# A two-layer attention and state-space block on one core: filter products, chunk outputs and key transposes laid out differently on the TensorE array

## The chip, the cores and the metric

The kernel runs on one core of one Trainium2 chip. The metric is device time in microseconds (us) of one execution. It is written by hand for each engine: every engine has its own list of instructions, and semaphores (`S["name"]`, counted up by `then_inc` and waited for by `wait_ge`) order them against each other.

## The reference

The input is 512 tokens of width 1024. A first layer modulates and normalises them, projects them, and mixes two branches: an attention branch (compressed, selected and window keys) and a state-space branch. Two further layers with neighbourhood attention and differential attention follow, then a last normalisation. The part that is changed lies in the first layer, above all in the state-space branch. There, 32 groups of 16 channels each carry a complex state of 64 values; the 512 tokens are cut into chunks of 8 tokens. In the kernel's form, each group's output is

```
y[group] = toe[group]^T . u[group]   (inside a chunk: a 128 x 128 block-triangular filter)
         + cl[group]^T  . st[group]  (what the state at the start of the chunk adds)
```

with u and st 128 x 64 (64 chunks). The filter blocks in `toe` come from small products kk[group] = b_st[group]^T . cl[group], 16 x 128, which DMAs then copy into a shifted pattern. The state `st` comes from v[group] = w[group]^T . u[group], a rotation, and a scan over the chunks.

## The kernel before

All matmuls of interest here have fp32 operands; the trace holds two records for each such matmul and one for each transpose. The bulk of the projections runs on a high and a low part of each operand (fp32r), three matmuls of 512 columns for each 128 x 128 piece of a weight.

TensorE's order around the change is written out (lines 1112 to 1264): the projections KV and KW (`proj_tok`, 96 matmuls each); 32 transposes of the state weights (L1119 to L1126); the 32 kk products (L1132 to L1137), whose outputs lie at partitions 0, 32, 64 and 96 in turn; the 64 v products (L1142 to L1149), in halves of 64 output partitions; the Q projection in four quarters, each waiting for its `p_lo`; two hidden layers of the key and value compression (hid); the y products, four for each group, in halves of 64 output partitions (L1163 to L1177); four blocks of the ZS projection with two small products between the third and the fourth; four blocks of the ZA projection, each followed by `queries_T`, which transposes queries and keys (L1206 to L1215); then the gated unit (GLU) and the first attention.

VectorE (DVE) has its own written order beside it: the tables of powers that feed kk and v, the statistics and rotation of the keys (L1836 to L1845), then the state: two halves of products with v from PSUM, each followed by `part_lo(14)` or `part_lo(15)`, which the third and fourth quarter of the Q projection wait for (L1853 to L1860), sums, two scans (L1863, L1864), and the states (L1865 to L1876). After that come the sums of squares of the queries, `part_lo(16)` and `part_lo(17)`, `queries(0)` and `queries(1)`, the hidden layer's activation and `part_lo(18)`, which the third ZS block waits for.

ScalarE (ACT) moves results out of PSUM (`activation` with Copy) and makes the high parts (`part_hi`). SyncE (SP) issues the DMAs in one order; the filter's pattern is written by `send_toe` (L442) as 32 DMAs, 8 for each of four tiles of 8 groups. `tmp_a`, `tmp_b`, `tmp_c` and `cq` are areas of SBUF used by several of these steps in turn. In the trace's names, `arena` holds `w_re`, `w_im`, `cl`, `u_in`, `tmp_a`, `tmp_b`, `tmp_c`, and `soft`, `gate_b` and `cols` hold parts of `toe`; `b_st` is in `soft`.

## Time and profile before

| | us |
|---|---|
| three runs | 3163.35, 972.14, 974.32 |
| median | 974.32 |
| profiled execution, its own time | 3163.35 |
| its span, first to last instruction | 3161.5 |
| PE busy in it | 3128.5 (99%) |
| DVE busy | 581.1 (18%) |
| ACT busy | 469.2 (15%) |
| POOL busy | 64.3 (2%) |

The profile is of the execution that took 3163.35 us; the two other runs of the same program took 972.14 and 974.32 us. Its times of DVE, ACT, POOL and of DMAs and its times of TensorE must therefore be read apart: which of them hold for an execution of 974 us is argued with the rows. Fractions of a microsecond within a group are read from the start of one piece of work to the start of the next, since matmuls overlap.

### The profile page before, as it was taken

What the parts mean: (1) busy time and instruction counts of PE and PEld (TensorE: products, weight loads), DVE (VectorE), ACT (ScalarE), POOL (GpSimd) and SP (SyncE); (2) the same over time, 40 slices, a digit from 0 to 9 for tenths busy, and PEclk for the clock granted to TensorE, in tenths of its full rate; (3) what the DMA queues carried; (4) which work ended last, traced back from release to release, by engine and by line L of the source; (5) the groups of instructions that cost most, each with busy time, mean ns of one, the idle gap of its engine ahead of it and who ended that gap; (6) DMA issues with size and microseconds to landing.
All of it is one profiled execution on the core that took longest, in us unless ns stands there. A gap on an engine that the chain in (4) does not pass through costs nothing.

```text
span 3161.5 us, 14396 instructions
## 1 busy us (share of the span) xinstructions
PE 3128.5 (99%) x5617; PEld 1683.1 (53%) x5617; DVE 581.1 (18%) x1174; ACT 469.2 (15%) x976; POOL 64.3 (2%) x82
## 2 busy tenths in 40 slices
PE   8999999999999999999999999999999999999998
PEld 3477455543445555555755555555555665555554
DVE  3322321212221110103300012011011320101200
ACT  3011001111231110102201013011110311101300
POOL 0000000002000000000000000000000000000000
DMA  5021110012000100100000001000010001001000
GB/s 206 14 43 50 29 62 20 30 53 80 0 1 7 39 26 27 40 27 25 27 27 27 27 27 45 15 25 13 27 47 27 19 27 31 22 27 40 21 0 27
DMA packets 94789, 104.68 MB, mean 33 GB/s; under 512 B 15937, under 2 KB 65089, under 8 KB 94722
## 3 DMA queue, kind: packets, MB, share of 16 engines
q1 hardware_dynamic: 90610, 87.67, 9.0%
q0 software_dynamic: 3824, 15.73, 1.5%
q8 instruction: 45, 0.74, 0.1%
q10 hardware_dynamic: 288, 0.36, 0.0%
q14 instruction: 22, 0.18, 0.0%
HBM read 98.37 MB, written 4.19 MB: 32 GB/s over the span
## 4 chain that ended last, share of the span: by engine, by line
PE 99%; DMA 0%; issue 0%; DVE 0%; ACT 0%; SPq 0%; DVEq 0%; POOLq 0%; POOL 0%; ACTq 0%
PE bank L1006 91%; PE bank L1326 2%; PE bank L1464 2%; PE bank L1306 2%; PE bank L1382 1%; PE bank L1372 0%; PE bank L1035 0%; PE bank L1125 0%; DMA ring<-in_w_ada 0%; PE bank L1212 0%; PE bank L1211 0%; PE bank L1289 0%; PE bank L1214 0%; SPq L448 0%; DVE k_lo L2191 0%
## 5 line engine op out<-in xcount | busy, mean ns | idle before, releaser
L1006 PE MATMUL bank<-w_hi,hT_hi 128*128 128x512 f32 x320 | 351.0, 1097 | 1.3 <-issue 1.0
L1006 PE MATMUL bank<-hT_hi,w_hi 128*128 128x512 f32 x320 | 351.0, 1097 | 0.0
L1006 PE MATMUL bank<-w_hi,hT_lo 128*128 128x512 f32 x320 | 350.7, 1096 | 0.0
L1006 PE MATMUL bank<-hT_lo,w_hi 128*128 128x512 f32 x320 | 350.6, 1096 | 0.0
L1006 PE MATMUL bank<-hT_hi,w_lo 128*128 128x512 f32 x320 | 350.1, 1094 | 0.0
L1006 PE MATMUL bank<-w_lo,hT_hi 128*128 128x512 f32 x320 | 349.0, 1091 | 0.0
L1006 PEld LDWEIGHTS bank<-w_hi,hT_hi 128*128 128x128 f32 x320 | 135.6, 424 | 129.7 <-issue 129.3
L1006 PEld LDWEIGHTS bank<-hT_lo,w_hi 128*128 128x128 f32 x320 | 138.0, 431 | 124.9 <-issue 124.3
L2059 DVE TENSOR_TENSOR w_lo<-ring,w_hi 128x1024 fp32r<-128x1024 f32 x80 | 97.9, 1225 | 575.5 <-ACT w_hi L866 575.5
L1006 PEld LDWEIGHTS bank<-w_hi,hT_lo 128*128 128x128 f32 x320 | 138.6, 433 | 122.0 <-issue 122.0
L1006 PEld LDWEIGHTS bank<-hT_hi,w_hi 128*128 128x128 f32 x320 | 135.7, 424 | 124.5 <-issue 123.5
L1006 PEld LDWEIGHTS bank<-w_lo,hT_hi 128*128 128x128 f32 x320 | 136.0, 425 | 123.7 <-issue 123.0
L1006 PEld LDWEIGHTS bank<-hT_hi,w_lo 128*128 128x128 f32 x320 | 136.0, 425 | 122.4 <-issue 122.4
L1006 PE MATMUL bank<-arena 128*64 128x64 f32 (+6 forms) x576 | 150.9, 673 | 0.3 <-PE bank L1006 0.2
L1006 PEld LDWEIGHTS bank<-arena 128*64 128x64 f32 (+2 forms) x576 | 83.0, 349 | 55.1 <-issue 44.5
L1006 PE MATMUL bank<-v,soft 128*128 128x128 f32 x256 | 112.1, 698 | 0.0
L1006 PEld LDWEIGHTS bank<-v,soft 128*128 128x128 f32 x256 | 109.3, 506 | 3.4
L1006 PE MATMUL bank<-o_hi,hT_r 128*128 128x512 f32 x96 | 105.4, 1098 | 0.0
L866 ACT ACTIVATE w_hi<-ring 128x1024 fp32r<-128x1024 f32 x80 | 84.3, 1056 | 140.7 <-PE bank L1006 140.6
L1006 PE MATMUL bank<-x_hi,ring_lo 128*128 128x512 f32 x104 | 89.1, 1094 | 0.0
L1006 PE MATMUL bank<-ring_lo,x_hi 128*128 128x256 f32 (+2 forms) x96 | 79.6, 829 | 0.0
L1006 PE MATMUL bank<-o_hi,a_hi 128*128 128x512 f32 x64 | 70.4, 1101 | 0.3 <-PE bank L1006 0.3
(313 smaller groups left out, 2912.3 us busy)
## 6 DMA issues: line engine op xcount, KB each, us to landing
ring<-in_w_in SPq DMA_DIRECT2D x66, 512.0 KB, 3.9
ring<-in_w_ada SPq DMA_DIRECT2D x4, 2048.0 KB, 14.1
ring<-in_w_in SPq DMA_DIRECT2D x4, 2048.0 KB, 8.3
bias_ring<-in_na_bias POOLq DMA_DIRECT2D x8, 1024.0 KB, 5.3
ring<-in_w_out SPq DMA_DIRECT2D x16, 512.0 KB, 3.4
ring<-in_w_out SPq DMA_DIRECT2D x2, 2048.0 KB, 7.8
bias_ring<-in_t_bias POOLq DMA_DIRECT2D x8, 448.0 KB, 3.7
x_t<-in_x SPq DMA_DIRECT2D x4, 512.0 KB, 6.0
```

The lines of the kernel that those rows point to most:

```text
L866: act.activation(w_hi[:, u % 4], raw_w[:, u % 4], ACT.Copy).then_inc(S["w_hi_ready"], 1)
L1006: return pe.matmul(out, lhsT, rhs, start=first, stop=last)
L1306: ins = pe.transpose(bank[u % 2][:, b * P:(b + 1) * P], src[:, b * P:(b + 1) * P], ident)
L1326: ins = pe.transpose(bank[k % 2][:, b * P:(b + 1) * P], prob1_of(k)[:, b * P:(b + 1) * P], ident)
L1382: ins = pe.transpose(bank[ROW_BANKS[i][b]][:, k * P:(k + 1) * P], xn[:, i % 2, (4 * b + k) * P:(4 * b + k + 1) * P], ident)
L1464: ins = pe.transpose(bank[m % 2][:, at_], prob2[:, m % 8, at_], ident)
L2059: dve.tensor_tensor(w_lo[:, u % 4], raw_w[:, u % 4], w_hi[:, u % 4].bitcast(fp32), SUB).then_inc(S["w_split"], 1)
```

## The change

Four things change, and nothing else in the program.

1. The kk products are made in eight groups of four, all with their output at partitions 0 to 15; each group is moved out by its own ACT copy of 16 partitions, into `cq` or `tmp_c`. Groups 16 to 31 come first. The v products take the real part first.
2. The tiles of `toe` are three (groups 0 to 15, 16 to 23, 24 to 31) and the pattern is written by 24 DMAs: 16 for the upper groups after four kk copies, 8 for the lower groups after eight. Since the upper kk lie in `tmp_c`, which the scans overwrite, DVE waits for those 16 DMAs ahead of the scans.
3. Each group's y takes two matmuls with all 128 output partitions. They have 128 columns (this group's and the next one's; the second half is overwritten by the next group's own result), and 64 for the last group of a bank.
4. `queries_T` makes the two transposes of keys as eight matmuls with the identity, of 64 output partitions each, that write every key block twice; ACT then moves them with one copy of 128 partitions in place of four of 64.

```diff
--- before.py
+++ after.py
@@ -192,7 +192,7 @@
         ksT = cut(rot_c, g=NG, t=T)
         kwT = cut(rot_s, g=NG, t=T)
         kT_all = cut(rot_cs, a=2 * NG, t=T)
-        kk = cut(cq[:, T:T + 8 * P], b=8, m=P)
+        kk_t = [cq[0:SC, T:T + GP * P], tmp_c[0:SC, :]]
         gate_bias = gate_b[0:1, :]
         mod_rows = soft[:, 0:2 * D]
         ada_late = [cut(arena[:, n * SLOT:(n + 1) * SLOT], k=KD, n=512) for n in range(2)]
@@ -242,10 +242,11 @@
 
         hid, hid_t = pw[:, 0:256], pw[:, 256:512]
         spent = cols[:, COLS["b_re"][0]:COLS["c_im"][1]]
-        toe = [cut(v, g=8, m=P) for v in (soft[:, 0:1024], soft[:, 1024:2048], gate_b[:, :], spent)]
+        toe = [(0, cut(soft[:, 0:2048], g=16, m=P)), (16, cut(gate_b[:, :], g=8, m=P)), (24, cut(spent, g=8, m=P))]
 
         def toe_of(g):
-            return toe[g // 8][:, g % 8, :]
+            g0, part = toe[0 if g < 16 else 1 if g < 24 else 2]
+            return part[:, g - g0, :]
 
         vdup = cut(spent[:, 0:512], k=2, g=NG, m=P)
         vblk = cut(spent[:, 512:1024], g=NG, f=256)
@@ -255,7 +256,7 @@
             "params_in", "x_in", "h_raw", "h_hi", "h_read", "p_hi", "p_lo", "p_used", "cl_moved", "k_stats", "k_rstd", "x_stats", "x_rstd", "xn_ready", "c_tanh", "c_silu", "ada_done", "mod_row",
             "tables_in", "za_ready", "gate_part", "gate_moved", "causal_in", "mod_cols", "h_lower", "qk_hi", "gate_done", "gate_ready",
             "xT_done", "xT_evac", "proj_done", "proj_evac", "w_free", "dt_ready", "zr_ready", "em_ready", "sin_ready",
-            "ang_ready", "wt_ready", "wt_done", "wt_evac", "cl_ready", "kk_done", "kk_evac", "toe_in",
+            "ang_ready", "wt_ready", "wt_done", "wt_evac", "cl_ready", "kk_done", "kk_evac", "toe_in", "toe_low",
             "zeroed", "u_out", "u_back", "hid_evac", "hidT_done", "hid_done", "hid_ready", "hid_tanh",
             "hid_gelu", "kc_done", "kc_ready", "kc_T", "kc_evac", "vc_done", "vblk_ready",
             "v_done", "state_ready", "y_done", "y_evac", "y_out", "y_back", "x_back", "q_stats", "q_rstd", "q_ready",
@@ -439,10 +440,11 @@
 
         @block.sync
         def _(sp):
-            def send_toe(a):
+            def send_toe(g0, part):
+                kk = cut(kk_t[g0 // 16], g=16, m=P)
                 for s in range(LC):
-                    sp.dma_start(toe[a][s * SC:(s + 1) * SC, :, (LC - 1 - s) * SC:P],
-                                 kk[32 * a:32 * a + SC, :, 0:(s + 1) * SC]).then_inc(S["toe_in"], 16)
+                    sp.dma_start(part[s * SC:(s + 1) * SC, :, (LC - 1 - s) * SC:P],
+                                 kk[:, g0 % 16:g0 % 16 + part.shape[1], 0:(s + 1) * SC]).then_inc(S["toe_in" if g0 else "toe_low"], 16)
 
             for i in range(NT):
                 sp.dma_start(x[:, i, :], io["x"][i * P:(i + 1) * P, :]).then_inc(S["x_in"], 16)
@@ -468,9 +470,11 @@
                                      u_dram[:, LC - 1 - s, :].rearrange("(g c) n -> c g n", c=SC)).then_inc(S["u_back"], 16)
                 elif c == CH_W1:
                     sp.wait_ge(S["zeroed"], 2)
-                    sp.wait_ge(S["kk_evac"], 2)
-                    for a in range(4):
-                        send_toe(a)
+                    sp.wait_ge(S["kk_evac"], 4)
+                    send_toe(*toe[1])
+                    send_toe(*toe[2])
+                    sp.wait_ge(S["kk_evac"], 8)
+                    send_toe(*toe[0])
                 elif c == CH_ZA:
                     sp.wait_ge(S["y_evac"], 4)
                     for t in range(LC):
@@ -708,9 +712,11 @@
                 act.wait_ge(S["wt_done"], n + 1)
                 dst = w_re if n < 4 else w_im
                 act.activation(dst[:, (n % 4) * 512:(n % 4 + 1) * 512], bank[4 + n % 4][:, :], ACT.Copy).then_inc(S["wt_evac"], 1)
-            for n in range(2):
+            for n in range(8):
                 act.wait_ge(S["kk_done"], n + 1)
-                act.activation(cq[:, T + n * 512:T + (n + 1) * 512], bank[4 + n][:, :], ACT.Copy).then_inc(S["kk_evac"], 1)
+                two, q = n % 2, (2 + n // 2) % 4
+                dst = cut(kk_t[q // 2], q=2, a=4, b=2, m=P)[:, q % 2, :, two, :]
+                act.activation(dst, cut(bank[4 + n % 4][0:SC, :], a=4, m=P), ACT.Copy).then_inc(S["kk_evac"], 1)
             part_hi(14)
             part_hi(15)
             for i in range(NT):
@@ -741,12 +747,7 @@
                 tok = slice(i * P, (i + 1) * P)
                 act.activation(qTn[:, :, tok], cut(bank[4][:, :], h=4, t=P), ACT.Copy)
                 act.activation(qTr[:, :, tok], cut(bank[5][:, :], h=4, t=P), ACT.Copy)
-                both = kT_all.rearrange("p (b g) t -> p b g t", g=NG)
-                for g in range(NG):
-                    src = cut(bank[6][g * HD:(g + 1) * HD, 0:2 * P], b=2, t=P)
-                    for u in range(2):
-                        ins = act.activation(both[u * HD:(u + 1) * HD, :, g, tok], src, ACT.Copy)
-                ins.then_inc(S["q_evac"], 1)
+                act.activation(kT_all[:, :, tok], cut(bank[6][:, :], a=2 * NG, t=P), ACT.Copy).then_inc(S["q_evac"], 1)
 
             for n in range(4):
                 act.wait_ge(S["y_done"], 4)
@@ -1128,23 +1129,24 @@
             pe.wait_ge(S["cl_moved"], 5)
             pe.wait_ge(S["cl_ready"], 2)
             cl3 = cut(cl, g=SG, m=(LC + 1) * SC)
-            pe.wait_ge(S["wt_evac"], 6)
-            for n in range(2):
-                for b in range(4):
-                    for a in range(4):
-                        g = 8 * a + 4 * n + b
-                        ins = mm(bank[4 + n][32 * a:32 * a + SC, b * P:(b + 1) * P], b_st[:, g, :], cl3[:, g, 0:P], True, True)
+            for n in range(8):
+                two, q = n % 2, (2 + n // 2) % 4
+                if n < 4:
+                    pe.wait_ge(S["wt_evac"], n + 5)
+                else:
+                    pe.wait_ge(S["kk_evac"], n - 3)
+                for a in range(4):
+                    g = 2 * (4 * q + a) + two
+                    ins = mm(bank[4 + n % 4][0:SC, a * P:(a + 1) * P], b_st[:, g, :], cl3[:, g, 0:P], True, True)
                 ins.then_inc(S["kk_done"], 1)
 
-            pe.wait_ge(S["wt_evac"], 8)
             pe.wait_ge(S["u_back"], 16 * LC)
             wr, wi = (cut(v, g=GP, m=P) for v in (w_re, w_im))
-            for part, w in enumerate((wi, wr)):
-                if part:
-                    pe.wait_ge(S["kk_evac"], 2)
+            for part, w in enumerate((wr, wi)):
+                pe.wait_ge(S["kk_evac"], 6 + 2 * part)
                 for g in range(GP):
                     for two in range(2):
-                        ins = mm(bank[6 - 2 * part + g // 8][two * SN:(two + 1) * SN, (g % 8) * NCH:(g % 8 + 1) * NCH],
+                        ins = mm(bank[4 + 2 * part + g // 8][two * SN:(two + 1) * SN, (g % 8) * NCH:(g % 8 + 1) * NCH],
                                  w[:, g, two * SN:(two + 1) * SN], u_in[:, 2 * g + two, :], True, True)
             ins.then_inc(S["v_done"], 1)
 
@@ -1160,7 +1162,8 @@
                 ins.then_inc(S["hid_done"], 1)
                 pe.wait_ge(S["hid_done"], s + 1)
                 pe.sem_inc(S["w_free"], 1)
-            pe.wait_ge(S["toe_in"], 16 * LC * len(toe))
+            pe.wait_ge(S["toe_in"], 16 * LC * 2)
+            pe.wait_ge(S["toe_low"], 16 * LC)
             pe.wait_ge(S["state_ready"], 1)
             st = cut(tmp_c, g=SG, n=NCH)
             for n in range(4):
@@ -1168,12 +1171,11 @@
                 for a in range(8):
                     g = 2 * (8 * q + a) + two
 
-                    out = bank[4 + n][:, a * NCH:(a + 1) * NCH]
-                    halves = [slice(h * SN, (h + 1) * SN) for h in range(2)]
-                    for half_ in halves:
-                        mm(out[half_, :], toe_of(g)[:, half_], u_in[:, g, :], True, False)
-                    for half_ in halves:
-                        ins = mm(out[half_, :], cl3[:, g, SC:SC + P][:, half_], st[:, g, :], False, True)
+                    w = NCH if a == 7 else 2 * NCH
+                    out = bank[4 + n][:, a * NCH:a * NCH + w]
+                    wide_ = lambda v: v.rearrange("p g n -> p (g n)")[:, g * NCH:g * NCH + w]
+                    mm(out, toe_of(g), wide_(u_in), True, False)
+                    ins = mm(out, cl3[:, g, SC:SC + P], wide_(st), False, True)
                 ins.then_inc(S["y_done"], 1)
 
             pe.wait_ge(S["hid_evac"], 2)
@@ -1211,7 +1213,9 @@
                     pe.transpose(bank[4][:, a * P:(a + 1) * P], q_tok[:, i, a * P:(a + 1) * P], ident)
                     pe.transpose(bank[5][:, a * P:(a + 1) * P], qr[:, i, a * P:(a + 1) * P], ident)
                 for b, kv in enumerate((kvs, kvw)):
-                    ins = pe.transpose(bank[6][:, b * P:(b + 1) * P], kv[:, i, 0:P], ident)
+                    for g in range(NG):
+                        for u in range(2):
+                            ins = mm(bank[6][u * HD:(u + 1) * HD, (2 * b + g) * P:(2 * b + g + 1) * P], kv[:, i, g * HD:(g + 1) * HD], ident, True, True)
                 ins.then_inc(S["q_T"], 1)
 
             def compressed_scores():
@@ -1860,6 +1864,7 @@
                 part_lo(14 + hb)
             tt(a0, a0, b0, ADD)
             tt(a1, a1, b1, SUB)
+            dve.wait_ge(S["toe_in"], 16 * LC * 2)
             settle(dve.tensor_tensor_scan(c0, r8, a0, 0.0, MUL, ADD))
             settle(dve.tensor_tensor_scan(c1, r8, a1, 0.0, MUL, ADD))
             tt(a0, c0, rot_c, MUL)
@@ -1897,7 +1902,7 @@
                 tt(lam[:, l:l + 1], lam_t[:, 2 * l + 1:2 * l + 2], lam_t[:, 2 * l:2 * l + 1], SUB)
                 ts(lam[:, l:l + 1], lam[:, l:l + 1], -(0.8 - 0.6 * math.exp(-0.3 * l)), None, ADD, ALU.bypass)
 
-            dve.wait_ge(S["toe_in"], 16 * LC * len(toe))
+            dve.wait_ge(S["toe_low"], 16 * LC)
             queries(0)
             queries(1)
 
```

On TensorE, the kk products and what stands around them (names as above; `wt_evac` counts ACT's copies of the transposed weights, `kk_evac` those of kk). Before:

```order
L1006 MATMUL bank<-arena,soft 16x128 [waits wt_evac,cl_ready,cl_moved]
L1006 MATMUL bank<-arena,soft 16x128 x31
L1006 MATMUL bank<-arena 64x64 [waits u_back,wt_evac]
L1006 MATMUL bank<-arena 64x64 x31
L1006 MATMUL bank<-arena 64x64 [waits kk_evac]
```

With the change, the last three of the eight groups of kk and the start of v:

```order
L1007 MATMUL bank<-arena,soft 16x128 [waits kk_evac]
L1007 MATMUL bank<-arena,soft 16x128 x3
L1007 MATMUL bank<-arena 64x64 [waits kk_evac,u_back]
L1007 MATMUL bank<-arena 64x64 x31
L1007 MATMUL bank<-arena 64x64 [waits kk_evac]
```

The number of kk and v products is the same; the kk products now stop for a copy after every four.

On TensorE, the start of the y products, before (`soft` is `toe`, the second matmul of a pair is with the state):

```order
L1006 MATMUL bank<-arena,soft 64x64 [waits hid_done,state_ready,toe_in]
L1006 MATMUL bank<-arena,soft 64x64
L1006 MATMUL bank<-arena 64x64 x2
L1006 MATMUL bank<-arena,soft 64x64 x2
L1006 MATMUL bank<-arena 64x64 x2
```

With the change:

```order
L1007 MATMUL bank<-arena,soft 128x128 [waits hid_done,state_ready,toe_low,toe_in]
L1007 MATMUL bank<-arena 128x128
L1007 MATMUL bank<-arena,soft 128x128
L1007 MATMUL bank<-arena 128x128
L1007 MATMUL bank<-arena,soft 128x128
```

Half as many matmuls stand there, each twice as wide in both directions.

On DVE, the first scan has one wait more. Before, and with the change:

```order
L1614 TENSOR_TENSOR ring_lo<-ring,o_hi 128x1024 [waits p_hi,vec_step]
L1584 TENSOR_TENSOR arena<-arena 128x1024
L1584 TENSOR_TENSOR arena<-arena 128x1024 [waits vec_step]
L1863 SCALAR_TENSOR_TENSOR arena<-soft,arena 128x1024 [waits vec_step]
L1864 SCALAR_TENSOR_TENSOR arena<-soft,arena 128x1024 [waits vec_step]
```

```order
L1618 TENSOR_TENSOR ring_lo<-ring,o_hi 128x1024 [waits p_hi,vec_step]
L1588 TENSOR_TENSOR arena<-arena 128x1024
L1588 TENSOR_TENSOR arena<-arena 128x1024 [waits vec_step]
L1868 SCALAR_TENSOR_TENSOR arena<-soft,arena 128x1024 [waits toe_in,vec_step]
L1869 SCALAR_TENSOR_TENSOR arena<-soft,arena 128x1024 [waits vec_step]
```

Nothing is moved on DVE; the wait stands behind the products with v and ahead of everything that makes the states.

## Rows read from the trace of the kernel before

**Rows 1.** The page's head and busy time of PE (share of the span, instructions).
```profile
span 3161.5 us, 14396 instructions
PE 3128.5 (99%) x5617; PEld 1683.1 (53%) x5617; DVE 581.1 (18%) x1174; ACT 469.2 (15%) x976; POOL 64.3 (2%) x82
```

**Rows 2.** Windows by step: start:end, length, busy us (instructions) per engine, clock, DMA.
```profile
core 0: us, PE busy (x) PEld busy (x) DVE busy (x) ACT busy (x) POOL busy (x), PEclk, DMA share, GB/s
...
192.54:276.00 83.46, 83.01 (x193) 77.78 (x192) 21.79 (x21) 12.94 (x22) 2.76 (x2) 1.00 0.07 25
276.00:289.10 13.10, 13.09 (x33) 8.02 (x33) 8.82 (x18) 4.49 (x8) 3.12 (x2) 1.00 0.50 161
289.10:295.66 6.56, 6.56 (x65) 3.85 (x64) 1.02 (x3) 1.20 (x2) 0.00 (x0) 1.00 0.00 0
295.66:308.83 13.17, 13.17 (x132) 13.10 (x129) 0.00 (x0) 0.60 (x1) 0.00 (x0) 1.00 0.32 46
308.83:387.90 79.07, 78.98 (x100) 40.62 (x96) 27.84 (x27) 3.37 (x5) 3.10 (x2) 1.00 0.05 8
388.15:441.30 53.15, 52.69 (x64) 18.53 (x64) 2.45 (x2) 2.79 (x6) 3.10 (x2) 1.00 0.24 79
441.44:467.80 26.36, 26.36 (x256) 26.29 (x256) 16.11 (x22) 2.01 (x3) 0.00 (x0) 1.00 0.23 81
468.57:552.10 83.53, 83.48 (x110) 44.41 (x109) 11.05 (x29) 8.93 (x16) 0.73 (x2) 1.00 0.09 25
552.35:647.70 95.35, 95.35 (x137) 51.63 (x138) 19.79 (x17) 16.92 (x34) 2.32 (x4) 1.00 0.09 32
```

**Rows 3.** Timeline: start, length, engine, line, out<-in; the compressed scores.
```profile
660.94 12.87 PE L1006 MATMUL bank<-arena 128*128 128x64 f32 x32
```

**Rows 4.** Groups by form, PE, whole run: xcount | busy us, mean ns.
```profile
L1006 PE MATMUL bank<-soft,arena 128*64 128x128 f32 x160 | 34.8, 652 | 0.0
```

**Rows 5.** Windows of DVE's steps: start:end, length, busy us per engine.
```profile
177.13:246.60 69.47, 69.17 (x148) 60.38 (x147) 26.54 (x24) 11.62 (x18) 2.76 (x2) 1.00 0.09 30
276.40:277.90 1.50, 1.50 (x6) 0.70 (x5) 1.38 (x2) 0.30 (x1) 0.00 (x0) 1.00 0.46 114
281.10:290.20 9.10, 9.10 (x36) 5.62 (x38) 8.46 (x18) 3.45 (x6) 0.01 (x1) 1.00 0.28 89
309.00:313.00 4.00, 4.00 (x6) 2.17 (x7) 3.53 (x6) 0.00 (x0) 0.00 (x0) 1.00 0.37 50
350.80:368.20 17.40, 17.40 (x22) 9.20 (x22) 16.85 (x14) 0.00 (x0) 0.00 (x0) 1.00 0.00 0
378.50:391.60 13.10, 12.77 (x17) 5.58 (x16) 4.89 (x4) 2.61 (x5) 3.10 (x2) 1.00 0.20 57
445.60:459.40 13.80, 13.80 (x138) 13.80 (x138) 13.22 (x17) 0.00 (x0) 0.00 (x0) 1.00 0.21 80
468.90:471.10 2.20, 2.20 (x4) 1.11 (x4) 1.89 (x6) 1.24 (x3) 0.00 (x0) 1.00 0.01 2
```

**Rows 6.** Timeline of DVE and ACT: single steps, idle before with its releaser.
```profile
281.14 0.69 DVE L1584 TENSOR_TENSOR arena<-arena,small 128x512 f32<-128x512 f32 x1 [3.33 <-POOL small L512]
...
330.00 1.22 DVE L1614 TENSOR_TENSOR ring_lo<-ring,o_hi 128x1024 fp32r<-128x1024 f32 x1 [17.23 <-ACT o_hi L663]
...
441.46 2.00 ACT L663 ACTIVATE a_hi<-ring 128x1024 fp32r<-128x1024 f32 x2
```

**Rows 7.** Groups of ACT, 267 to 350 us and 572 to 580 us.
```profile
L710 ACT ACTIVATE arena<-bank 128x512 f32<-128x512 f32 x8 | 4.8, 598 | 8.7 <-PE bank L1125 8.7
...
L713 ACT ACTIVATE cq<-bank 128x512 f32<-128x512 f32 x2 | 1.2, 598 | 5.4 <-PE bank L1006 5.4
...
L748 ACT ACTIVATE arena<-bank 64x256 f32<-64x256 f32 x4 | 1.5, 378 | 0.0
```

**Rows 8.** Timeline of SP's issues; DMA issues with size and us to landing.
```profile
296.50 10.95 SPq L444 DMA_DIRECT2D soft<-cq  x16
307.49 5.10 SPq L444 DMA_DIRECT2D gate_b<-cq  x8
...
soft<-cq SPq DMA_DIRECT2D x2, 64.0 KB, 2.3
```

## The prediction

> **What bounds the kernel now.** I read the page's head first. The profiled execution has a span of 3161.5 us and an own time of 3163.35; PE is busy 3128.5 us of it [rows 1], so in that execution TensorE alone sets the end. But the median of the runs is 974.32, 2189 us less, and PE's work cannot fit into that at this pace. The durations of DVE, ACT, POOL and the DMAs I take as they stand; those of TensorE have to be divided.
>
> By how much: 3128.5 us in at most 974.3 is a factor of at least 3.21. The Q projection is 96 matmuls of 512 columns in 79.07 us [rows 2], 0.824 us each; the granted clock is 1.00 in every window, the 2.4 GHz level, and 512 columns at one per cycle would be 0.213 us, a factor of 3.86. I take 3.8, since 3128.5/3.8 = 823 leaves 151 us for the start and the waits, and keep 3.21 for the range. The Trainium skill (TensorE: Matmul & The Clock Gate, "Seeing it yourself") says that the clock has been seen stuck at a quarter. By a factor of 4.0 instead of 3.8 the sum below would be 0.8 us less; the granted clock in this trace does not show such a state, though the pitch resembles it.
>
> With 3.8, other engines can be late. So the views that matter are the windows by step, first of PE [rows 2], then of DVE [rows 5]: the reader is to see that the two lists have nearly the same length between the KV projection and the third ZS block.
>
> **What each edit adds on PE, in the profiled pace.** (a) kk: 32 matmuls in 6.56 us [rows 2] are 0.205 each. The 32 transposes, one record each of 128 columns, take 13.10 us, 0.41 a record; a matmul of two records that uses the array alone should take 0.82. kk runs four times faster because neighbouring products have outputs at different partitions. With all at partitions 0 to 15 this goes: 32 x 0.82 = 26.3, so +19.7. (b) y: 128 matmuls in 26.36 us are 0.206 each; two halves run side by side. With 128 output partitions a record costs 0.40 even for 64 columns (32 records in 12.87 us [rows 3]); PEld is busy 26.29 of 26.36 us in the y window [rows 2], so loading weights costs as much as the columns do. Widening to 128 columns adds nearly nothing to that (0.41), but neither does it save: 128 records x 0.41 = 52.5, +26.1. (c) keys: each of four `queries_T` loses 2 records of 0.41 and gains 16 of 64 output partitions and 128 columns, 34.8/160 = 0.22 [rows 4]: 3.5 - 0.8 = 2.7, four times 10.8. Together +56.6 us; an execution like the profiled one, where PE hides all else, would go from 3163 to about 3220. Divided by 3.8: kk +5.2, y +6.9, keys +2.8, 14.9 in all.
>
> **What of it is hidden.** Time A is the start of KV on PE. DVE has just made `part_lo(8)` then, by the order of the lists (an estimate: it must also wait for ACT there).
> - DVE: 26.5 us busy to the squares of the second keys, 1.5, 3.3 of waiting for POOL [rows 6], 9.1: keys done at A+40.4. Then 3.5 (first half of v) and 1.2 (`part_lo(14)`, rows 6 too): A+45.1; half two, 4.1: A+49.2; then 17.4 to the states: A+66.6 [rows 5].
> - PE: KV and KW 83.46/3.8 = 22.0; the transposes 3.4, but their eight ACT copies take 4.8 [rows 7]: A+26.8; kk 1.7, v 3.5: A+32.0; two quarters of Q, 10.4: A+42.4. There it waits for `part_lo(14)`, 2.7 us. Then Q 10.4 and hid 14.0: A+69.5, later than the states. y 6.9: A+76.4.
>
> With the change kk ends 5.2 later, so the first two quarters end at A+47.6, past A+45.1: of the 5.2, 2.7 are hidden and 2.5 are seen. y starts at A+72.0 and ends at A+85.8.
>
> Second place: DVE goes on at A+66.6 with 4.9 of squares, then needs high parts that ACT makes only after hid (2.0 us [rows 6] for two), so `part_lo(17)` is there at about A+73.2; 0.7 of small work, queries 13.8, the hidden activation 2.2 [rows 5], `part_lo(18)` 1.2: A+91.1. PE, from A+76.4 with two ZS blocks of 5.2, is at A+86.8 and waits 4.3. Changed, DVE is 2.5 later (A+93.6, from hid), PE is at A+96.2 and waits no more: the shift is 96.2 - 91.1 = 5.1. The keys come behind it and are fully seen, +2.8: **7.9 us**. Handovers between engines are not in these sums, and DVE's list has more of them, so the waits of PE are rather longer than 2.7 and 4.3; I take 7.
>
> **What costs nothing, and under what cover.** The copies of kk: eight of 16 partitions, some 0.6 each by [rows 7], against 0.9 us of PE for each group; they stay behind PE, and the last adds about 0.7 ahead of v's second part, between nothing and that. If PE did not pace them, 8 x 0.6 = 4.8 would replace 1.2. The key copies: four of 0.38 become one of 0.60 [rows 7], 0.9 saved on ACT, four times, while PE is in the next ZA block of 5.2 us; nothing, unless ACT is last there. SP's 32 issues at 0.64 [rows 8] become 24; neither sets y's start. **The new wait**: DVE may not scan before 16 DMAs have landed. Four kk copies are done at about A+31.5; 16 x 0.68 [rows 8] and 2.3 for landing give A+44.7. The scans stand at A+49.2 + 2.5 = A+51.7, so 7 us are to spare. The lower tile's eight DMAs of twice the bytes end near A+55, y starts at A+72. Behind a late scan are the states and then y on PE.
>
> **Rivals.** Each is a time of 974.3 plus its price.
> - *No wait hides anything.* PE is never behind DVE in an execution of 974 us. Against it: the 151 us that are left for waits. Price 14.9 at factor 3.8, 17.6 at 3.21: 989 to 992.
> - *Issue sets the narrow matmuls.* The profiled pace never shows a record shorter than 0.10 us (kk, v and y alike [rows 2]), and 3.8 times faster would be 0.027. Between these ends, if a record costs f whatever it does, y goes from 256f to 128 x 0.108 = 13.8; above f = 0.054 the change gains there. At f = 0.103: y -12.6, kk +0.3, keys 4 x (1.65 - 0.22) = +5.7, in all -6.6: 968. At f = 0.06: y -1.6, kk +3.1 hidden mostly, keys +3: 976. I take 972. The Trainium skill (same page, "Wait — 56ns, not 53.3ns?") gives about 62 ns of sequencer time for a matmul where decoding is not in hardware and never under 25; by the first, y would be 15.9 before and 13.8 after. No row here shows it.
> - *A wait costs more than its length.* If PE comes back from a wait at the 1.2 GHz level, the block behind it takes up to 5.2 more. Before has two such waits, after has none: up to -10.4 + 7 = -3.4, 971. For it: the equal lists. Against: the granted clock is 1.00 in all windows, but PE never waited here. The skill's page ("What's actually happening") says that the throttled state is the default and activity releases it.
> - *Slower by over 2%.* The whole stage runs at the 1.2 GHz level, because PE stops often in it: then the factor there is 1.9, DVE is never late, and all 56.6 us are seen as 29.8: 1004. It decides from a factor below 2.9 (56.6/19.5). Against it, the average factor is at least 3.21. The new wait belongs here only if the DMAs took three times as long.
> - *It does not do what it says*: neighbouring kk products overlap although their outputs share partitions. Then +9.7, and less by the waits: about 978, inside the forecast.
>
> **Chances and numbers.** A change of under 2% (19.5 us) is about what a measurement of this kernel can tell from none. Forecast, +3 to +11: 0.56. No wait hides: 0.15. Issue: 0.14. Costlier waits: 0.10. Over 2% slower: 0.04. Over 2% faster, by nothing that I can name: 0.01. The time is 974.3 + 7 = 981. The range goes down to 970, which takes in the costlier waits and most of the issue case, and up to 990, with most of the case where nothing is hidden. Faster by over 2% 0.01, within 0.94, slower 0.05.
>
> **What would show it.** In the changed profile, if PE's pace there is the one of an execution near 980: kk 7 us long with 0.2 us to a product, y near 14; in the profiled pace of before, 26 and 52. Before the third quarter of Q and before the third ZS block there is no wait for DVE; the scan does not wait for a DMA. It is wrong if y is shorter than before, if the toe DMAs land after DVE's sums, or if DVE, not PE, is what the ZA blocks wait for (then even 7 is too much).

## The result and the profile after

The changed kernel takes 986.78 us (median of 4 runs, 986.62 to 987.02); the kernel before 973.23, the median of four executions of which one is that of 3163 us; the ratio leaves that one out. The ratio is 1.0143, 95% interval [1.0124, 1.0164]: slower, by less than 2%. The prediction said 981 and 970 to 990.

The profile of before was of that long execution. A second look at the same program (experiment 1) gave one of 971.54 us with a span of 969.7; the profile after is compared with that one. The head of the page, first before in that execution, then after (own time 988.49):

```profile
span 969.7 us, 14396 instructions
...
PE 922.5 (95%) x5617; PEld 722.8 (75%) x5617; DVE 579.0 (60%) x1174; ACT 454.0 (47%) x976; POOL 66.6 (7%) x82
```

```profile
span 986.7 us, 14239 instructions
...
PE 940.5 (95%) x5545; PEld 738.2 (75%) x5545; DVE 579.3 (59%) x1174; ACT 454.2 (46%) x970; POOL 66.7 (7%) x82
```

Beside [rows 1], DVE, ACT and POOL are what they were and PE went from 3128.5 to 922.5: the other engines' durations could be carried over, PE's had to be divided, and by 3.39, not by 3.8. PE gained 18.0 us of busy time with 72 fewer matmul records.

Where, by step. The windows of before in that execution (start:end, length, busy us of PE, PEld, DVE, ACT, POOL, granted clock, DMA share): KV to the transposes, kk, v, Q, (hid is left out), y, the four ZS blocks, the four ZA blocks with `queries_T`, the first GLU piece, the compressed scores.

```profile
69.50:97.85 28.35, 27.72 (x225) 27.14 (x224) 26.90 (x25) 16.43 (x29) 3.60 (x4) 1.00 0.55 134
97.85:99.72 1.87, 1.87 (x64) 1.66 (x65) 0.00 (x0) 1.43 (x3) 1.87 (x1) 1.00 1.06 363
99.72:103.60 3.88, 3.88 (x132) 3.81 (x128) 3.26 (x6) 0.60 (x1) 0.42 (x1) 1.00 0.49 150
103.60:126.28 22.68, 22.38 (x100) 17.98 (x97) 21.71 (x30) 3.59 (x5) 0.00 (x0) 1.00 0.38 53
...
141.70:150.04 8.34, 7.80 (x257) 7.63 (x257) 6.91 (x11) 2.00 (x3) 3.83 (x3) 1.00 0.72 255
150.31:174.97 24.66, 24.29 (x113) 19.03 (x110) 19.81 (x41) 9.53 (x16) 0.73 (x2) 1.00 0.31 86
174.97:202.09 27.12, 27.12 (x138) 22.37 (x139) 18.92 (x16) 16.45 (x34) 0.62 (x1) 1.00 0.24 88
202.09:205.52 3.43, 3.43 (x10) 1.52 (x9) 0.69 (x1) 2.67 (x7) 1.70 (x4) 1.00 0.93 305
205.52:209.04 3.52, 3.52 (x34) 3.52 (x32) 0.69 (x1) 0.69 (x1) 0.00 (x0) 1.00 1.07 291
```

The same windows after, without the last:

```profile
69.60:97.73 28.13, 27.68 (x225) 27.14 (x223) 26.86 (x25) 16.19 (x29) 3.42 (x4) 1.00 0.57 135
97.73:104.83 7.10, 7.10 (x66) 6.13 (x65) 4.36 (x8) 5.19 (x10) 2.47 (x1) 1.00 0.65 206
104.83:108.71 3.88, 3.88 (x130) 3.81 (x129) 3.57 (x10) 0.59 (x1) 0.00 (x0) 1.00 0.27 57
108.71:131.39 22.68, 22.35 (x100) 17.97 (x97) 17.89 (x20) 3.61 (x5) 0.00 (x0) 1.00 0.32 43
...
147.05:161.36 14.31, 14.31 (x128) 14.31 (x129) 12.64 (x17) 2.00 (x3) 2.87 (x1) 1.00 0.43 149
161.59:185.90 24.31, 24.01 (x112) 19.11 (x110) 14.29 (x34) 9.66 (x16) 0.73 (x2) 1.00 0.32 86
185.90:216.92 31.02, 31.02 (x193) 24.93 (x194) 19.59 (x17) 14.07 (x25) 1.51 (x3) 1.00 0.23 78
```

Three steps grew: kk 1.87 to 7.10 (+5.2), y 8.34 to 14.31 (+6.0), the ZA blocks 27.12 to 31.02 (+3.9). v and Q, which were to give back a wait, are 3.88 and 22.68 in both. KV with the transposes, hid and the ZS blocks differ by 0.2 to 0.35. The start of the GLU pieces went from 202.09 to 216.92, +14.8 for a sum of +15.1. The granted clock is 1.00 in all of these windows, before and after (the 2.4 GHz level), so none of it is the clock.

The spans of the two profiled executions differ by 17.0, so another 2.2 us arise behind the start of GLU, where nothing was changed. There the changed one has a stretch at a granted clock of 0.50 (the 1.2 GHz level) that experiment 1's has not, behind 7.9 us in which PE was idle for 1.9:

```profile
899.90:906.70 6.80, 6.54 (x42) 5.03 (x44) 2.65 (x18) 5.08 (x19) 0.78 (x1) 0.50 0.67 224
```

The profiles of the experiments below repeat this: from the start of GLU to the end they take 767.6 to 767.8 us or, with such a stretch more (3.4 to 6.8 us near 585 or 900), 769.3 to 769.8; only experiment 8, which changes work there, takes less. Executions of before with a mean granted clock of 0.990 or more lie mostly at 971.5 to 972.0 us, the others at 973.2 to 976.0; four of the five changed ones had 0.992 and took 986.6 to 987.0. Like with like, the change costs 15 us, as the windows add up to; the 13.6 between the medians is a little low.

What PE waited for, from KV to the start of the ZA blocks, before and after (us in total, times, longest):

```profile
PE bank L1006 <- PE bank L1006: 1.2, 4, 0.3
PE bank L1006 <- DMA ring<-in_cmp_w_v: 0.8, 1, 0.8
PE bank L1006 <- issue: 0.5, 1, 0.5
PE bank L1006 <- ACT arena L710: 0.2, 1, 0.2
```

```profile
PE bank L1007 <- PE bank L1007: 1.2, 4, 0.3
PE bank L1007 <- DMA ring<-in_cmp_w_v: 1.0, 1, 1.0
```

That is all in this execution: 2.7 us before, none of it put down to DVE. But the 0.5 for "issue" is a pause inside y, and it covers a wait for DVE. The profiles of experiments 3, 4 and 5 have the same y step without that pause, 7.6 us long (experiment 4: y, then the ZS blocks):

```profile
142.79:150.41 7.62, 7.62 (x257) 7.55 (x257) 6.22 (x10) 2.00 (x3) 3.82 (x3) 1.00 0.79 279
150.68:176.05 25.37, 24.29 (x113) 19.03 (x110) 20.49 (x42) 9.51 (x16) 0.73 (x2) 1.00 0.30 83
```

and there the third ZS block waits 0.8 us for DVE, for the hidden activation (`hid_ready`, the tile `pw`):

```profile
162.85 2.13 PE L1001 MATMUL bank<-x_hi,a_hi 128*128 128x512 f32 x8 [0.78 <-DVE pw L1914]
```

From the start of y to the start of the ZA blocks it is 33.2 to 33.3 us in experiments 1, 3, 4, 5 and 7, with the pause or without, which fits DVE setting that end; after the change it is 38.9. So the y edit costs 6.65 of array time (7.89 to 14.54, from the start of y to that of ZS), and 1.1 of it is hidden there.

### The profile page after: what moved, and what is told of

Same layout as the page of the kernel before. It is cut to its first block, busy times and chain, and to the rows that moved or that the text cites. A ratio compares the mean times of both kernels' runs of the same rounds, so it can differ in the third digit from the quotient of the medians.

```text
span 986.7 us, 14239 instructions
## 1 busy us (share of the span) xinstructions
PE 940.5 (95%) x5545; PEld 738.2 (75%) x5545; DVE 579.3 (59%) x1174; ACT 454.2 (46%) x970; POOL 66.7 (7%) x82
## 4 chain that ended last, share of the span: by engine, by line
PE 83%; DVE 6%; ACT 4%; DMA 4%; issue 3%; DVEq 0%; SPq 0%; POOL 0%; POOLq 0%; ACTq 0%; PEldq 0%
PE bank L1007 77%; DVE ring L2009 2%; PE bank L1330 2%; ACT ring L917 2%; DMA ring<-in_w_in 1%; PE bank L1310 1%; DMA ring<-in_w_ada 1%; DMA ring<-in_cmp_w_v 1%; PE bank L1468 1%; ACT soft L924 1%; PE bank L1386 1%; ACT w_hi L867 0%; PE bank L1126 0%; PE bank L1376 0%; ACT hT_hi L849 0%
## 5 line engine op out<-in xcount | busy, mean ns | idle before, releaser
L1007 PE MATMUL bank<-w_hi,hT_hi 128*128 128x512 f32 x320 | 125.3, 392 | 1.3 <-issue 1.0
L1007 PE MATMUL bank<-hT_hi,w_hi 128*128 128x512 f32 x320 | 125.8, 393 | 0.0
L1007 PE MATMUL bank<-hT_lo,w_hi 128*128 128x512 f32 x320 | 124.6, 389 | 0.0
L1007 PE MATMUL bank<-w_lo,hT_hi 128*128 128x512 f32 x320 | 124.6, 389 | 0.0
L1007 PE MATMUL bank<-hT_hi,w_lo 128*128 128x512 f32 x320 | 124.5, 389 | 0.0
L1007 PE MATMUL bank<-w_hi,hT_lo 128*128 128x512 f32 x320 | 124.5, 389 | 0.0
L1007 PEld LDWEIGHTS bank<-w_hi,hT_hi 128*128 128x128 f32 x320 | 60.1, 188 | 14.7 <-issue 2.6
L1007 PEld LDWEIGHTS bank<-hT_lo,w_hi 128*128 128x128 f32 x320 | 60.1, 188 | 12.7
L1007 PEld LDWEIGHTS bank<-w_lo,hT_hi 128*128 128x128 f32 x320 | 60.1, 188 | 12.6
L1007 PEld LDWEIGHTS bank<-w_hi,hT_lo 128*128 128x128 f32 x320 | 60.1, 188 | 12.2
L1007 PEld LDWEIGHTS bank<-hT_hi,w_lo 128*128 128x128 f32 x320 | 60.1, 188 | 12.1
```

The lines of the kernel that those rows point to most:

```text
L1007: return pe.matmul(out, lhsT, rhs, start=first, stop=last)
```

## The experiments

Theory A, formed on these rows: the kernel is bound by PE through the whole stage, nothing hides, and each edit costs what its records cost on the array, because products whose outputs lie at the same partitions can't overlap. Rival B: one part (the new wait, the copies of 16 partitions, the DMAs) costs beyond the array. Rival C: a record's price is issue or moving columns. ("Record" is a matmul record of the trace; an fp32 matmul has two.) Times are medians; ratios are to the kernel before in the same set of runs (973.77 for 1 to 4, 973.69 for 5 to 8, 974.12 for 9 and 10).

**1. Before again.** No edit.

> The kernel before, unchanged, for a trace of an execution near 973 us. Both theories: 973 +- 1 us, ratio 1.000. My theory (PE is nearly always last in this stage, so nearly all added array time is seen): y takes about 7.5 us, kk about 1.9 us, and TensorE waits less than 2 us in all between the KV projection and the third ZS block. Rival (the waits that I predicted are there, and the 13.5 us come from larger terms): 2 to 3 us of wait ahead of the third quarter of Q and about 4 ahead of the third ZS block.

973.7 us, 1.000 [0.999, 1.001]. Its profile is the one used above.

**2. The y edit alone.**

```diff
-                    for half_ in halves:
-                        mm(out[half_, :], toe_of(g)[:, half_], u_in[:, g, :], True, False)
...
+                    mm(out, toe_of(g), wide_(u_in), True, False)
+                    ins = mm(out, cl3[:, g, SC:SC + P], wide_(st), False, True)
```

> The kernel before with the y edit alone (two matmuls of 128 x 128 for a group). If PE is always last: +7 us (980). If a wait of 4 us behind it hides part: +3 (976). If records were bound by issue: below 973.

979.67, 1.0064 [1.0050, 1.0078], +5.9. The y step is 14.31 long (141.86 to 156.17), the ZS blocks 24.3 in place of 24.7 (the wait for DVE is gone), all else as before.

**3. The kk edit alone**, with its three toe tiles, its copies and the new wait of DVE.

```diff
-                        ins = mm(bank[4 + n][32 * a:32 * a + SC, b * P:(b + 1) * P], b_st[:, g, :], cl3[:, g, 0:P], True, True)
+                    ins = mm(bank[4 + n % 4][0:SC, a * P:(a + 1) * P], b_st[:, g, :], cl3[:, g, 0:P], True, True)
...
+            dve.wait_ge(S["toe_in"], 16 * LC * 2)
```

> The kernel before with the kk edit alone (eight groups at partitions 0 to 15, three toe tiles, the scan's wait for DMAs). If PE is always last: +5 us (978). If the wait ahead of the third quarter of Q hides half: +2.5 (975.7). If the new wait on DVE binds: over +8.

978.46, 1.0049 [1.0035, 1.0062], +4.7. kk is 7.09 long (97.62 to 104.71); v and Q behind it are as long as before.

**4. The keys edit alone.**

```diff
-                    ins = pe.transpose(bank[6][:, b * P:(b + 1) * P], kv[:, i, 0:P], ident)
+                    for g in range(NG):
+                        for u in range(2):
+                            ins = mm(bank[6][u * HD:(u + 1) * HD, (2 * b + g) * P:(2 * b + g + 1) * P], kv[:, i, g * HD:(g + 1) * HD], ident, True, True)
```

> The kernel before with the keys edit alone (eight identity matmuls for two transposes, one ACT copy for four). PE always last: +2.8 us (976). If ACT is last in a ZA block: 0 or less.

978.21, 1.0049 [1.0031, 1.0068], +4.4. The ZA blocks take 31.0 (176.05 to 207.06), 1.0 more for each, and PE waits for nobody between them. The three add up to +15.0, against +13.6 for all together; the intervals, 1.2 to 2 us to each side, don't tell these apart, and at the start of GLU the sum of the shifts is 14.3 against 14.7 (each less the shift of its KV).

**5. kk at one place, without copies, tiles and wait.** Before, all kk products written to partitions 0 to 15.

```diff
-                        ins = mm(bank[4 + n][32 * a:32 * a + SC, b * P:(b + 1) * P], b_st[:, g, :], cl3[:, g, 0:P], True, True)
+                        ins = mm(bank[4 + n][0:SC, b * P:(b + 1) * P], b_st[:, g, :], cl3[:, g, 0:P], True, True)
```

> The kernel before with every kk product written to partitions 0 to 15 (three quarters of the products overwrite one another, so the filters for three quarters of the groups are wrong; timing only); still two groups, two ACT copies, 32 DMAs, no new wait. If the lost side-by-side running of products explains the kk edit: kk takes 7.0 us instead of 1.9, and the total is +5 (978.5), as for the whole kk edit. If the copies, waits and DMAs of the kk edit cost: under +2.

978.11, 1.0048 [1.0031, 1.0065]: +4.4, against +4.7 in experiment 3. PE's timeline (start, length; the last row of a timeline can be cut short by its window), kk in this kernel:

```profile
98.72 7.15 PE L1006 MATMUL bank<-arena,soft 128*16 128x128 f32 x64 [0.17 <-ACT arena L710]
105.80 0.92 PE L1006 MATMUL bank<-arena 128*64 128x64 f32 x24
```

0.11 us a record, as in the changed kernel; v starts at 105.80, 7.08 after kk. So it is the place of the outputs alone. It is the partitions and not the address: here four products share one address, in the changed kernel each has its own, and the pace is the same. What else that edit brought (six more copies, 24 DMAs for 32, the wait) costs nothing that these runs can tell: rival B falls for kk.

**6. The change with 64 columns in y.**

```diff
-                    w = NCH if a == 7 else 2 * NCH
+                    w = NCH
```

> The changed kernel with the y products at 128 output partitions but 64 columns. If the loading of 128 columns of weights sets the pace (my theory): y stays at 14.3 us, total 986.8 +- 1. If the array's columns set it: y falls to about 7.3 us and the total to 980.

986.34, 1.0138 [1.0116, 1.0159], as the change itself. Its y step is 14.32 long. Half the moving columns give nothing back.

**7. Before with 32 columns in y.**

```diff
-                        mm(out[half_, :], toe_of(g)[:, half_], u_in[:, g, :], True, False)
+                        mm(out[half_, :], toe_of(g)[:, half_], u_in[:, g, 0:NCH // 2], True, False)
...
```

> The kernel before with y in halves of 64 output partitions, but over 32 of the 64 columns of u and of the state (half of the outputs of the state-space branch are then not computed; timing only). If the array's columns set the 0.033 us of a record: y falls from 8.3 to about 4.5 us, total 969.5. If a record costs what its issue or its 64 columns of weights cost: y stays at 8 us, total 973.7.

973.72, 0.9998 [0.9988, 1.0009]; y is 8.40 long, of which 0.65 is a pause like that of experiment 1 (0.54 there). In halves, too, fewer than 64 columns give nothing.

**8. The opposite of the change elsewhere.** If halves are cheaper, then the compressed scores, which the kernel before makes with 128 output partitions and 64 columns, should gain from them, and so should four small value products.

```diff
-                        ins = mm(bank[i // 2][:, o:o + 2 * NCMP], qTn[:, h, i * P:(i + 1) * P], kcT[:, h // 2].rearrange("p u j -> p (u j)"), True, True)
+                        for u in range(2):
+                            ins = mm(bank[i // 2][u * SN:(u + 1) * SN, o:o + 2 * NCMP], qTn[:, h, i * P + u * SN:i * P + (u + 1) * SN],
+                                     kcT[:, h // 2].rearrange("p u j -> p (u j)"), True, True)
...
```

> The kernel before with the compressed scores (16 products of 128 output partitions and 64 columns, 3.5 us) and four small value products cut into halves of 64 output partitions that run side by side, as y is in the kernel before. By the pace of y, 64 records at 0.033 us are 2.1 us: total -1.5 (972.2). If DVE is last after the scores: no change (973.7).

971.34, 0.9974 [0.9965, 0.9983]: 2.4 us faster than before, faster than both kernels. PE's timeline before (experiment 1), then here:

```profile
205.52 3.68 PE L1006 MATMUL bank<-arena 128*128 128x64 f32 x32
209.04 7.09 PE L1006 MATMUL bank<-arena,ring 128*128 128x512 f32 x16
```

```profile
205.64 2.08 PE L1006 MATMUL bank<-arena 128*64 128x64 f32 x64
207.65 4.56 PE L1006 MATMUL bank<-arena,ring 128*128 128x512 f32 x10
```

From the start of the scores to the start of what follows, 3.52 us became 2.01 with twice the records. That is 1.5 of the 2.4, whose interval is 1.7 to 3.4. From the start of y to that of ZA, where the value products lie, the profile has 32.8 us for 33.3.

**9. Before with y in quarters** of 32 output partitions.

```diff
-                    halves = [slice(h * SN, (h + 1) * SN) for h in range(2)]
+                    parts = [slice(h * 32, (h + 1) * 32) for h in range(4)]
...
```

> The kernel before, with each y product in quarters of 32 output partitions: 512 records of 32 x 64 in place of 256 of 64 x 64; the result is the same. The question is what sets a record's 0.033 us in halves, since halving its moving columns did not change it. If each record costs that whatever it holds (issue), y takes 512 x 0.033 = 16.8 us, 8.4 more than now: about 982. If the cost goes with the output partitions whose weights are loaded, 32 in place of 64, a record takes about 0.016, y stays at 8.3 and the time at 973.7. The kk products before, 16 output partitions and 0.029 us a record, speak for the first. I expect 981 to 982.

979.83, 1.0056 [1.0037, 1.0076], +5.7. y is 14.65 long (142.65 to 157.30), 0.0286 a record on average, where 16.8 or 8.3 were expected. PE's timeline:

```profile
142.65 0.32 PE L1006 MATMUL bank<-arena,soft 128*32 128x64 f32 x8 [0.33 <-PE bank L1006]
142.75 0.32 PE L1006 MATMUL bank<-arena 128*32 128x64 f32 x8
...
147.49 0.32 PE L1006 MATMUL bank<-arena 128*32 128x64 f32 x3 [2.68 <-issue]
```

The average misleads. While PE works, eight records start every 0.11 us: 0.014 each, half of what a record costs in halves, so the array's own time is about the same (512 x 0.014 = 7.2 us, 256 x 0.029 = 7.5). But three pauses, 5.1 us together, break them up, in which PE waits for nothing that the profile shows (2.7, 0.7 and 1.7 us), and behind the first the granted clock falls to the 1.2 GHz level. Two windows, one of 128 records there, one of 128 behind the next pause:

```profile
147.49:151.00 3.51, 3.51 (x128) 3.43 (x128) 3.37 (x5) 0.00 (x0) 0.00 (x0) 0.52 0.56 214
151.80:153.80 2.00, 1.96 (x128) 1.81 (x128) 1.90 (x4) 0.00 (x0) 0.00 (x0) 1.00 0.04 8
```

So y is longer for the 5.1 us of pauses and the 1.5 of the slower clock; without them some 8 us are left. The pauses come after 139, 128 and 128 records; the one pause of 0.54 us in the y of experiment 1 comes after 139 too. The trace's packets of the instruction queue are of 16 KB and start 4.2, 3.7 and 3.7 us apart there. That PE ran out of instructions fits this, and is argued, not shown. Rival C in the form that each record costs 0.03 to issue falls; in the form that a long run of short records is not supplied faster than about 0.03 each, it stands.

**10. Before with 128 columns in y's halves.**

```diff
-                        mm(out[half_, :], toe_of(g)[:, half_], u_in[:, g, :], True, False)
+                        mm(out[half_, :], toe_of(g)[:, half_], wide_(u_in), True, False)
...
```

> The kernel before, with the y products still in halves of 64 output partitions but over 128 columns (this group's and the next one's, as the change has them; the surplus is overwritten, the result is the same). 256 records as before. If a record costs 0.033 us whatever it moves, nothing changes: 973.7. If 128 columns at one per cycle of 2.4 GHz (0.053 us) show in each record, y is 256 x 0.053 = 13.6 us, 5.3 more: 979. If two halves stream their columns at the same time, a pair needs 0.053, less than the 0.066 that it takes now, and nothing changes either. With records of 32 and 64 columns equal, I expect no change, 974, at 0.7; 979 at 0.3.

977.02, 1.0035 [1.0024, 1.0046], +2.9, against my expectation of no change. PE's timeline:

```profile
142.18 0.44 PE L1006 MATMUL bank<-arena,soft 128*64 128x128 f32 x4 [0.30 <-PE bank L1006]
142.42 0.42 PE L1006 MATMUL bank<-arena 128*64 128x128 f32 x4
142.64 0.42 PE L1006 MATMUL bank<-arena,soft 128*64 128x128 f32 x4
```

y is 13.31 long, 0.052 a record on average. Where they have 128 columns, four records start every 0.22 us, 0.055 each against 0.029 for 64 columns; the last group of each bank still has 64. y grew by 5.0 us, and 4.6 are seen at the start of GLU in its profile. Its span is 974.9, 5.2 above experiment 1's, and both profiles have 767.7 us behind the start of GLU. Nine of the eleven executions of before in this set had a mean clock of 0.989 or less and took 973.9 or more, five of the eight here had 0.990 or more, so the 2.9 between the medians is too little.

## Why the prediction was right, and where it was wrong

The time, 986.8, lies in the stated range of 970 to 990 and outside the forecast of +3 to +11. It lies in the range only because this was stretched to take in most of the first rival; the sum that gave 981 had the costs right and the hiding wrong. That part is luck.

**What bounds the kernel** was right: TensorE, and other engines' durations could be taken as they stood. DVE's chain came out as summed: `part_lo(14)` was put at A+45.1 and ends at A+44.8 (KV starts at 69.50).

```profile
113.03 1.23 DVE L1614 TENSOR_TENSOR ring_lo<-ring,o_hi 128x1024 fp32r<-128x1024 f32 x1
```

**What each edit adds on PE** was right in sum and near in its terms: kk +5.2 said, +5.2 measured; y +6.9 said, +6.0 in the windows, where before's y has the pause of 0.54, and +6.65 against a y without it; keys +2.8 said, +3.9; 14.9 said, 15.1 in the windows. The mechanism is the one of the text: experiment 5 shows it for kk, 6 and 8 for y. Keys were put too low: a block of 16 records takes 1.02 us from its start to the next step's, 0.064 each instead of 0.058, and there is another 0.1 ahead of it, where PE changes from transposes to matmuls. Inside the block two records start every 0.11 us, 0.055 each, so the surplus is at its ends:

```profile
192.69 0.27 PE L1214 MATMUL bank<-cons,cq 128*128 128x128 f32 x1
192.90 1.09 PE L1007 MATMUL bank<-cons,arena 128*64 128x128 f32 x16
193.92 0.96 PE L1007 MATMUL bank<-x_hi,z_hi 128*128 128x512 f32 x3
```

**What of it is hidden** is the step that failed. It said that PE waits 2.7 us for `part_lo(14)` and 4.3 ahead of the third ZS block, and that the change fills these waits, so that 7 of 14.9 us are seen. The first wait does not exist, so kk's +5.2 is seen whole; the second is 0.8 us where y has no pause, and 1.1 of y is hidden there.

Two things went into that. The first is the factor: Q takes 22.68, 79.07 divided by 3.49, and KV and KW took 24.5, by 3.41. So the second quarter of Q ends at A+45.3 (114.78), just behind DVE's A+44.8, not 2.7 ahead of it. In the same way PE comes to the third ZS block at A+91.3 (experiment 4, without the pause) and not at A+86.8. DVE's chain to `hid_ready` starts with the end of hid, which is later for the same reason; in experiment 1 it ends at A+92.2:

```profile
161.29 0.42 DVE L1917 TENSOR_TENSOR pw<-pw 128x256 f32<-128x256 f32 x1
```

I had taken 3.8 from the pitch of 512 columns and a guess of 151 us for idle time; PE is idle for 47. By the lower end that I kept for the range, 3.21, the same working leaves nothing of the first wait and 1 us of the second, near what was measured; the sum should have been made at both ends.

The second is a reading of the code: in ZS `proj_T` waits at the start of the third block for `hid_ready`, but for `p_lo` only after eight products with the high part. DVE's late `part_lo(18)`, which my sum waited for, stands beside these:

```profile
161.64 1.22 DVE L1614 TENSOR_TENSOR ring_lo<-ring,a_hi 128x1024 fp32r<-128x1024 f32 x1
```

```profile
161.77 2.13 PE L1006 MATMUL bank<-x_hi,a_hi 128*128 128x512 f32 x8
163.74 0.62 PE L1006 MATMUL bank<-x_hi,ring_lo 128*128 128x512 f32 x2
```

It starts 0.1 before PE's third block, ends at 162.86, and is first wanted at 163.7. So the first rival, *no wait hides anything*, is what happened, but for about 1 us: its lower end was 974.3 + 14.9 = 989, and the time is 986.8.

**What costs nothing** was right. The new wait: the scan starts behind DVE's sums, with no idle time, at 124.93.

```profile
121.28 1.23 DVE L1618 TENSOR_TENSOR ring_lo<-ring,o_hi 128x1024 fp32r<-128x1024 f32 x1 [1.52 <-ACT o_hi L667]
122.42 2.48 DVE L1588 TENSOR_TENSOR arena<-arena 128x1024 f32<-128x1024 f32 x2
124.93 2.29 DVE L1868 TENSOR_TENSOR_SCAN arena<-soft,arena 128x1024 f32<-128x1024 f32 x1
```

The DMAs it waits for were issued from 102.12 to 113.39:

```profile
102.12 6.10 SPq L446 DMA_DIRECT2D gate_b<-arena  x8
108.26 5.13 SPq L446 DMA_DIRECT2D cols<-arena  x8
```

So even with the 2.3 us to landing of [rows 8] they were in 9 us before. The eight copies take 0.59 each and stand behind PE, as said:

```profile
99.69 0.59 ACT L719 ACTIVATE arena<-bank 16x512 f32<-16x512 f32 x1 [0.29 <-PE bank L1007]
```

DVE itself now waits for ACT in this place, 1.5 us in the row above; it has that room, since PE is later too.

**The other rivals.** *Issue sets the narrow matmuls* falls. It needed 0.054 us a record to make y a gain; quarters run at 0.014. The long execution had it already: the 0.10 that the prediction took as the shortest record there is an average, and in that trace kk's records start in fours, mostly within 13 ns, 0.42 us from one four to the next. The Trainium skill (TensorE: Matmul & The Clock Gate, "Wait — 56ns, not 53.3ns?") gives about 62 ns for a matmul where decoding is not in hardware, and never under 25 from start to start. Neither holds for the records here that lie at different partitions: in quarters they start 6 to 8 ns apart in groups of four, 0.014 us each on average and 0.028 for a matmul of two. The measurement decides. *A wait costs more than its length* has no case in this stage: the one wait is under 1 us, and the granted clock behind it is 1.00. Experiment 9 shows the case itself, behind a pause of 2.7 us. *The whole stage at 1.2 GHz* falls with the granted clock of 1.00. *It does not do what it says* falls with kk's 7.10.

## What to carry to other kernels

Small fp32 products should go to different output partitions in turn (four places of 16, or two halves of 64). Fewer matmuls with wider outputs were not cheaper here, and moving 64 columns in place of 128 with 128 output partitions saved nothing. Splitting has a limit that is not the array's: 64 records in a row ran without a pause, 256 with none or one of 0.5 us, 512 with 5.1 us of pauses. An average over a step hides such pauses; look for gaps before calling it the price of a record.

When a profile is of an unusual execution, keep apart what scales and what does not, and take the factor for the step in question from its bounds: a hidden cost that is there at one end of the bounds and gone at the other should not be counted whole. Before counting a wait, look in the code for what stands between the start of the step and the instruction that waits. And when two kernels differ by 1%, compare executions with the same granted clock.

## What the runs showed of the hardware

Microseconds for one fp32 record (two for each matmul), from start to start while PE works without a pause:

| output partitions x columns | next record's outputs | us a record | from |
|---|---|---|---|
| 128 x 128 | same | 0.112 | y after |
| 128 x 64 | same | 0.112, 0.110 | 6; scores before |
| 16 x 128 | same | 0.111 | kk after, 5 |
| 16 x 128 | four places in turn | 0.029 | kk before, over the whole step |
| 64 x 128 | two halves in turn | 0.055 | 10; keys after, without their ends |
| 64 x 64 | same | 0.059 | four records ahead of the value products, before and after |
| 64 x 64 | two halves in turn | 0.029 | y before (0.033 over the step, with its pause); 8 (0.031 over the step) |
| 64 x 32 | two halves in turn | 0.029 | 7 |
| 32 x 64 | four quarters in turn | 0.014 | 9 |

One reading fits all of it. The GLU piece of eight fp32 records of 512 columns takes 3.43 us, 0.43 each, where the Q projection's records of 512 columns take 22.68/96 = 0.236. So an fp32 record moves 128 columns in about 0.107. If loading its weights costs as much for each output partition, the longer of the two sets the record, and records at different partitions run side by side, then the table comes out as 0.107, 0.107, 0.107, 0.027, 0.053, 0.053, 0.027, 0.027, 0.013. The runs show each row. That it is the loading of weights that sets 128 x 64 was argued from what is left, not shown; for 64 x 32 a least length of some 0.056 for each two or four records side by side would do as well.

In the execution of 3163 us PE took 3.4 to 3.7 times as long for its steps (v 3.39, KV and KW 3.41, y 3.46 against the 7.62 without a pause, Q 3.49, kk 3.51, scores 3.66) with a granted clock of 1.00 in every window, while DVE, ACT and POOL kept their pace. Why is open: no run here took that long again.
